# Differential attention: the two softmax halves weighed and turned by products with diagonal matrices

## The reference, cut to what matters

```python
def _diff_attend(q, k, v, lam):
    s = jnp.einsum('bhcqd,bhckd->bhcqk', q, k).astype(jnp.float32) * (A_DH ** -0.5)
    p = jax.nn.softmax(s, axis=-1)
    w = p[:, :, 0] - lam * p[:, :, 1]
    return jnp.einsum('bhqk,bhkd->bhqd', w.astype(v.dtype), v)
```

## Time and profile before

| | |
|---|---|
| time, median of 3 runs | 3147.98 us (3142.18 to 3152.9) |
| time of the profiled execution | 3148.47 us |
| its span, from the first to the last instruction | 3146.6 us |
| mean granted TensorE clock over the span | 0.963 |
| PE busy | 2731.3 us (87%) |
| PEld busy | 1984.0 us (63%) |
| DVE busy | 1403.3 us (45%) |
| ACT busy | 930.7 us (30%) |
| attention stage, first score to start of the last sum | layer 0: 391.8 to 652.3 us; layer 1: 2062.4 to 2272.0 us |
| period of one head | layer 0: 33.6 us; layer 1: 27.3 us |

### The profile page before, as it was taken

How to read it: one execution, slowest core, us unless ns; L and a number is a source line. 1 busy time by engine, 2 the same in 40 slices (tenths; PEclk the granted TensorE clock), 3 DMA queues, 4 the chain that set the end, 5 groups by cost and what they waited for, 6 DMA issues and landing times. The chain is left out here.

```text
span 3146.6 us, 40804 instructions
## 1 busy us (share of the span) xinstructions
PE 2731.3 (87%) x15578; PEld 1984.0 (63%) x15578; DVE 1403.3 (45%) x2560; ACT 930.7 (30%) x1615; POOL 0.2 (0%) x4
## 2 busy tenths in 40 slices
PE   5999999889998998987888878788789988987886
PEld 3887766567877766444444558766578886444444
DVE  5466655567454844111111566655474554111112
ACT  4223244433343332100000253344434443100001
POOL 0000000000000000000000000000000000000000
PEclk9999999999999998999999989999889998999999
DMA  6113411043111542999999322621062236999995
GB/s 230 73 67 122 162 41 40 27 167 121 67 67 41 205 164 103 428 429 398 416 428 429 119 87 87 237 81 53 26 245 92 81 134 248 428 429 428 428 429 217
DMA packets 59494, 635.11 MB, mean 202 GB/s; under 512 B 7854, under 2 KB 9840, under 8 KB 11376
## 3 DMA queue, kind: packets, MB, share of 16 engines
q1 hardware_dynamic: 59376, 633.55, 50.0%
HBM read 632.48 MB, written 1.05 MB: 201 GB/s over the span
## 5 line engine op out<-in xcount | busy, mean ns | idle before, releaser
L191 PE MATMUL ps<-rounded,rounded 128*128 128x256 f32 (+1 forms) x1856 | 640.8, 345 | 71.4 <-DVE rounded L182 36.8
L192 PE MATMUL ps<-rounded,rounded 128*128 128x256 f32 (+1 forms) x1856 | 629.8, 339 | 0.0
L193 PE MATMUL ps<-rounded,rounded 128*128 128x256 f32 (+1 forms) x1856 | 629.5, 339 | 0.0
L2219 PE MATMUL ps<-high_arena,low_arena 128*64 128x256 f32 x4288 | 497.9, 387 | 126.3 <-DMA high_arena<-in_e_w 97.9
L2219 PEld LDWEIGHTS ps<-high_arena,low_arena 128*64 128x64 f32 x4288 | 314.6, 139 | 331.3 <-DMA high_arena<-in_e_w 113.6
L182 DVE TENSOR_TENSOR rounded<-low_arena,rounded 128x1024 fp32r<-128x1024 f32 (+3 forms) x344 | 369.2, 1097 | 239.1 <-ACT rounded L178 234.8
L191 PEld LDWEIGHTS ps<-rounded,rounded 128*128 128x128 f32 x1856 | 361.7, 195 | 116.6 <-DVE rounded L182 35.6
L192 PEld LDWEIGHTS ps<-rounded,rounded 128*128 128x128 f32 x1856 | 362.0, 195 | 35.4 <-issue 0.5
L193 PEld LDWEIGHTS ps<-rounded,rounded 128*128 128x128 f32 x1856 | 361.2, 195 | 36.3
L178 ACT ACTIVATE rounded<-low_arena 128x1024 fp32r<-128x1024 f32 (+3 forms) x344 | 313.9, 950 | 195.5 <-PE ps L193 111.2
L167 PE MATMUL ps<-high_arena 128*128 128x256 f32 (+3 forms) x1072 | 264.3, 399 | 42.2 <-DVE high_arena L547 12.9
(11 more groups left out here) (383 smaller groups left out, 2743.9 us busy)
## 6 DMA issues: line engine op xcount, KB each, us to landing
high_arena<-in_e_w SPq DMA_DIRECT2D x201, 2048.0 KB, 25.4
low_arena<-in_d_wm SPq DMA_DIRECT2D x48, 1024.0 KB, 4.8
high_arena<-in_d_modlater SPq DMA_DIRECT2D x40, 1024.0 KB, 4.9
low_arena<-in_d_wml SPq DMA_DIRECT2D x32, 1024.0 KB, 4.9
low_arena<-in_d_wh SPq DMA_DIRECT2D x16, 1536.0 KB, 6.8
low_arena<-in_d_wa SPq DMA_DIRECT2D x16, 1536.0 KB, 6.6
low_arena<-in_d_wo SPq DMA_DIRECT2D x8, 1024.0 KB, 4.8
low_arena<-in_d_modfirst SPq DMA_DIRECT2D x3, 2048.0 KB, 29.6
```

The source lines that it names most:

```text
L191: pe.matmul(out, l_hi, r_hi, start=(k == 0), stop=False)
L192: pe.matmul(out, l_lo, r_hi, start=False, stop=False)
L193: last = pe.matmul(out, l_hi, r_lo, start=False, stop=(k == n - 1))
L2219: last = pe.matmul(K.ps[h * S:h * S + S, 4 * s + i, 0:HF], xg[s][:, k, :], w[:, k, h * HF:h * HF + HF], start=(k == 0), stop=(k == KC - 1))
```

## The change

The scaled sum `w` is no longer made on VectorE. VectorE makes two diagonal matrices of 128 x 128 per tile instead, each the identity times the factor of one half. The turn becomes, for each block of 128 keys, two float32 products accumulated in PSUM: the block of `pr` half c is the stationary operand, diagonal c the moving one. Since the turn now reads `pr` itself, ScalarE's wait before overwriting `pr` is on `turned` of the same tile number instead of on `weighted`.

```diff
-        w = [K.f(124 + 2 * s, NTOK) for s in range(2)]
+        diag = [K.f(124 + s, 2 * P).rearrange("p (c n) -> p c n", c=2) for s in range(2)]
...
                 pe.wait_ge(weighted, u * nq + n + 1)
                 pe.wait_ge(copied, u * nq + n)
                 for b in range(qtiles[n][1] // P):
-                    last = pe.transpose(K.ps[:, 6, b * P:b * P + P], w[n % 2][:, b * P:b * P + P], K.ident)
+                    last = accumulate(pe, K.ps[:, 6, b * P:b * P + P], lambda c: pr[n % 2][:, c, b * P:b * P + P],
+                                      lambda c: diag[n % 2][:, c, :], 2)
                 last.then_inc(turned, 1)
...
                 act.wait_ge(maxed, u * nq + n + 1)
-                act.wait_ge(weighted, u * nq + (n - 1) if n else u * nq)
+                act.wait_ge(turned, u * nq + (n - 1) if n else u * nq)
...
-                    ch.then(v.tensor_scalar(w[n % 2][:, 0:keys], pr[n % 2][:, 0, 0:keys], st[:, n, 3, 0:1], None, ALU.mult))
+                    ch.then(v.tensor_scalar(diag[n % 2][:, 0, :], K.ident, st[:, n, 3, 0:1], None, ALU.mult))
                     ch.wait()
-                    v.scalar_tensor_tensor(out=w[n % 2][:, 0:keys], in0=pr[n % 2][:, 1, 0:keys], scalar=st[:, n, 3, 1:2],
-                                           in1=w[n % 2][:, 0:keys], op0=ALU.mult, op1=ALU.add).then_inc(weighted, 1)
+                    v.tensor_scalar(diag[n % 2][:, 1, :], K.ident, st[:, n, 3, 1:2], None, ALU.mult).then_inc(weighted, 1)
```

## The result

| | before | after |
|---|---|---|
| median | 3147.27 us (4 runs, 3142.18 to 3152.9) | 3187.55 us (4 runs, 3184.5 to 3188.69) |
| profiled execution's span | 3146.6 us | 3186.9 us |
| mean granted clock | 0.963 | 0.965 |
| PE / PEld / DVE / ACT busy | 2731.3 / 1984.0 / 1403.3 / 930.7 us | 2771.4 / 2042.8 / 1377.6 / 929.9 us |

The changed kernel is slower: ratio 1.0125, 95% interval 1.0109 to 1.0141, 40 us. The forecast was 3191.9 us (3181 to 3204). VectorE lost 26 us of work and PE gained 40 us.

A forecast was written before the change was run, and what follows sets the result against it. The prediction took PE to bound the attention stage, with VectorE's relief counting only where PE waits. 22.3 + 19.0 + 1.6 + 0.5 = 43.4 us on the profiled 3148.5 us gave 3191.9 us (+1.4%), range 3181 to 3204.

The forecast's parts named there:

- layer 0, seven heads: Typical heads of layer 0: 12 blocks at +0.339 us less 0.89 us of slack, 3.18 us per head, +22.3 us.
- layer 1, seven heads: Typical heads of layer 1: 8 blocks at +0.339 us with no slack, 2.71 us per head, +19.0 us.
- The block's price: PE's turn of one block: 0.448 us instead of 0.109, +0.339 us, from four records of 0.112 us.
- Counted as one record: Rival on PE's turns: one record per product, a block +0.115 us, 10 us in all, 3158 us; chance 0.03.
- The slack: PE's waits between turn(0) and the end of turn(3): 0.89 us per head in layer 0, zero in layer 1.
- The sign that the prediction named for more slack than it had read: In layer 0, score(3) still starting when exps(2) ends would mean PE had more slack than the 0.89 us read.
- the rival on VectorE: VectorE's factors set each tile's pace, so both layers' heads get shorter: 25 us faster, 3123 us; chance 0.02.
- VectorE's part: Two new operations of about 0.28 us each per tile; factors ready 0.66 us earlier at 512 keys, 0.26 at 256.
- The changed wait: ScalarE's exps of tile n waiting for the turn of n - 2 adds nothing; costed at nothing.
- The last heads: Last head of each layer, where PE waits for the factors: +1.6 us in layer 0, +0.5 us in layer 1.
- the clock rival: Half-clock windows of both last heads go, mix 1.9 us shorter in layer 0: about 3187 us; chance 0.14.
- the two branches: Layer 1's last head: ends 1.7 us earlier if the clock stays full, 2.1 us later if it falls.

The follow-up runs named there:

- e5: The kernel after with pr and the diagonals in rounded form, so each product is one record instead of two: 3155.3 us, ratio 1.0019.
- e3: The kernel after with three products for each block instead of two (half 0 added twice, so another output): 3203.1 us, ratio 1.0169.
- e2: The kernel after with one product for each block instead of two (half 1 left out of the output): 3152.3 us, ratio 1.0012.
- e1: The kernel after, but PE turns half 0 of pr by one transpose per block; VectorE still makes the diagonals, weighing left out: 3139.5 us, ratio 0.997.
- e4: The kernel before with only ScalarE's wait changed, on turned instead of weighted: 3147.0 us, ratio 0.9999.
- e6: The kernel before with the change in the last head of each layer alone: 3145.1 us, ratio 0.9988.
- e9: The kernel after with the two moves of e8: 3164.5 us, ratio 1.0055 to the kernel before.
- e10: e8 with the change in the last head of each layer alone: 3120.6 us, ratio 0.9919 to the kernel before.
- e7: The kernel before with layer 1's second query projection piece moved from behind turn(0) to ahead of score(1): 3136.4 us, ratio 0.9959.
- e8: As e7, with mix also cut in two so its copied part runs while the last tile is being copied: 3115.9 us, ratio 0.99 to the kernel before.

## Why the prediction came out

The terms of the sum against the two profiled executions. "Elsewhere" is all outside the stretches from the first score to the last sum of squares.

| term | predicted | measured |
|---|---|---|
| layer 0, seven heads | +22.3 | +21.6 |
| layer 1, seven heads | +19.0 | +18.8 |
| last head, layer 0 | +1.6 | -0.1 |
| last head, layer 1 | +0.5 | -1.6 |
| elsewhere | 0 | +1.5 |
| sum | +43.4 | +40.2 |

Six of layer 0's seven heads are 2.98 us longer each; the seventh, which leads into the last head, is 3.75 us longer. That "elsewhere" came out near the 0 of the prediction is in part luck: against the kernel before, the same stretches of the other kernels that leave nothing out take between 1 us more (e5) and 8 us less (e8).

**The block's price** was right: 0.112 us per record, read from the Hyena stage, is what the records of the turn take in the kernel after and in e3. That a float32 product is two records and a transpose is one carries the whole result. Counted as one record, the forecast would have been 3158 us. The two attention stages have 640 records of turns, as forecast, but listed at the helper's line L167 and not at the line of the turn.

**The slack** was right in place and a little small in size. For a head of layer 0 it is 1.09 us (after, e2, e3), not 0.89. The missing 0.2 us is a price in the kernel before: I took 0.109 us for every transpose, but rows 3 show that only the turn without a wait is that fast. The turns after a wait for `w` took 0.66 us for four records and 0.44 for two, so their first step was 0.165 us; three such turns are 0.17 us that the change also removed. The row was there, and I read it only for its start. The sign that the prediction named for more slack than it had read did not appear: score(3) starts 17.2 us into the head (482.83), and ScalarE's exponentials of tile 2 end at 15.0 us in both kernels, so PE comes to score(3) 2.3 us after they are out, as forecast. The other slips are small: (1.02 - 0.38) / 3 is 0.213 and not 0.215, and the 25 us of the rival on VectorE count eight heads of each layer where the other sums count seven.

**VectorE's part** was right: 0.28 us for each new operation (280 and 286 ns), and no wait of a typical head's turn on VectorE is left. e1 shows what the relief is worth by itself, 0.27 us a head in layer 0 and nothing in layer 1.

**The changed wait** costs nothing (e4), for the reason given: the copy ahead of it waits for the same turn.

**The last heads** are the step that failed in size. I put them at +2.1 us: in layer 0 with the half clock kept, in layer 1 near the middle between full and half clock. They came to -1.7, which is the clock rival: the stretch of half clock that in the kernel before starts during the last long wait and covers what follows was gone in both layers. In layer 0 the last turn starts 1.40 us later in the head, not 0.8, and mix 1.88 us later; the -0.1 comes out because mix then takes 1.94 us less. In layer 1 the last turn starts 0.67 us earlier, as forecast, and mix takes 1.99 us where it took 3.78. For layer 1 the two branches had been worked out, and the measured -1.63 us is the one at full clock (-1.7). With this in place of the middle, the sum is 39.6 us, and the rival's own time, about 3187 us, is nearer to the measured 3187.6 than the forecast is. For layer 1 the cause is supported by e6 and e9: with a wait of 0.7 us no half clock followed (after, e6, e9, e10), with 2.7 us it did in the kernel before, e4 and e7. It is not a sure rule: in e8 the wait was 2.71 us and none followed, and a wait of 1.6 us was followed by 3.4 us at half clock in e5 and by none in e2. In e1 the wait was 2.05 us and half clock started during it. Whether it also matters that the work ahead is products instead of transposes was not separated from the shorter wait in layer 1; in layer 0 products alone did not keep the clock up: e2 and e5 turn by products, waited 2.5 us, and had 3.4 and 6.8 us at half clock. There the wait of 2.0 us went both ways (after and e10 full, e6 and e9 half for 3.4 us). Why the clock stayed up in the kernel after is therefore open.

## What to carry to other kernels

Before moving work to TensorE, count records, not products: here a float32 product of 128 columns is two records of 0.112 us and a transpose one of 0.109, so weighing and turning a block by two products quadruples PE's time for it. Taking 1.85 us of work in a head from VectorE is worth little when PE waits for that work only about 0.3 us in a head; read the waits by place and compare the added work with the slack that lies between the two points that it moves, not with the sum of idle time. The same reading finds the real gain: work that is ready, moved ahead of a wait that PE already has (e8, -1.0%, three quarters of it in the attention stages).

## What was not expected of the hardware

A rounded product of 128 columns (e5) is one record but starts no faster than a record of the float32 product, 0.11 us, although rounded products of 512 columns step by 0.23 us and would give 0.06 by proportion (those of 256 columns in layer 1 step by 0.12 us in e7, close to proportion). The runs do not show what holds it; the weight load of 128 columns that each one has is the common part, and it was not varied. So rounding halves the records of a narrow product and nothing more.

Stages that were not touched differ by several microseconds between executions of different kernels, both ways. From the last sum of squares in layer 0 to the first score in layer 1, where none of these kernels has an edit:

```profile
652.11:2062.36 1410.25, 1224.91 (x7058) 882.37 (x7056) 630.62 (x1151) 376.76 (x615) 0.00 (x0) 0.96 0.56 225
```

```profile
647.77:2051.87 1404.10, 1218.28 (x7059) 876.80 (x7057) 630.34 (x1151) 376.60 (x615) 0.00 (x0) 0.96 0.56 226
```

The first is the kernel before, the second e8: 6.15 us less for the same work, with PE busy 6.6 us less. In the clock records of the traces the stretch has 116 us at half clock in the first and 102 in the second; e1 has 1404.4 us with 109. In e4, which has the same heads as the kernel before and the same 116 us at half clock, it is 1406.9, and e10 has 1409.1 us with only 106. So part of it may go with how much half clock falls into the stretch, which no run varied by itself, and part is open. The extra gain of e1 and e8 over their heads can't be explained further here. It is the reason why a few microseconds of a kernel's total say less than the distance of two heads.
